# A hybrid sparse-attention encoder in float32: the masks of two tiles built between attention's rows

## What is computed

```python
h = rms_norm(x, gains[0]);  z = h @ w_in        # q k v, indexer q k w, conv B C x, gates A B
score = sum_h wi[h] * relu(qi[h] . ki) ;  score = where(key_chunk <= q_chunk, score, -inf)
_, idx = lax.top_k(score, topk)                 # 256 keys for a prompt row, 40 for a sample row
kg, vg = k[idx], v[idx]
p = softmax(q . kg / 8 over the chosen keys);  o = p @ vg        # 8 query heads, 2 key heads
m = sigmoid(ga) * (o @ w_attn_out) + sigmoid(gb) * ((cb * conv3(cc * cx)) @ w_conv_out)
x = x + rms_norm(m @ w_o, gains[1])
x = x + rms_norm(square(relu(rms_norm(x, gains[2]) @ w_up)) @ w_down, gains[3])
```

## Time and profile before

| | |
|---|---|
| time, median of 3 runs | 3700.87 us (3700.28 to 3704.8) |
| profiled execution: time, span | 3699.1 us, 3697.3 us |
| TensorE matmuls busy | 3375.3 us, 91% |
| VectorE busy | 1903.4 us, 51% |
| ScalarE busy | 721.0 us, 20% |
| GpSimd busy | 1185.1 us, 32% |
| granted TensorE clock, mean | 0.948 of full speed |
| values matmuls (line 623) | 197.0 us in 368 |
| logits matmuls (line 594) | 169.9 us in 704 |

### The profile page before, as it was taken

The page is one execution under the profiler, slowest core; times in us unless marked ns, Lnnn a source line. Parts: engine busy times, 40 slices in busy tenths (PEclk is TensorE's granted clock), DMA queues, the critical chain, the costliest instruction groups (busy, mean ns, idle before and its releaser), DMA issues.

```text
span 3697.3 us, 48934 instructions
## 1 busy us (share of the span) xinstructions
PE 3375.3 (91%) x19604; PEld 3201.4 (87%) x19604; DVE 1903.4 (51%) x3006; ACT 721.0 (20%) x1113; POOL 1185.1 (32%) x497
## 2 busy tenths in 40 slices
PE   3989997999979999999749899979998799999996
PEld 2989996669969999999739899956798799999996
DVE  4249997644174242424372599976442733323244
ACT  2330112541121010101123201125402200101010
POOL 6013331004334443434350133310044344334441
PEclk9989997999979999999869899979999799999998
DMA  4111222012211111112121112220132111111121
GB/s 165 47 57 42 71 91 98 23 42 99 93 65 46 42 44 45 45 45 91 38 90 53 54 44 76 93 87 24 42 105 100 59 43 43 45 45 45 40 93 59
DMA packets 75359, 233.95 MB, mean 63 GB/s; under 512 B 12816, under 2 KB 25456, under 8 KB 73712
## 3 DMA queue, kind: packets, MB, share of 16 engines
q1 hardware_dynamic: 33552, 122.57, 11.0%
q10 hardware_dynamic: 41696, 109.88, 8.0%
HBM read 176.37 MB, written 56.05 MB: 63 GB/s over the span
## 4 chain that ended last, share of the span: by engine, by line
PE 70%; DVE 23%; issue 3%; ACT 2%; ACTq 1%; POOL 1%; DMA 0%; SPq 0%; DVEq 0%; POOLq 0%
PE PS L410 52%; DVE PASS L1268 11%; PE PS L476 5%; PE PS L623 4%; PE PS L594 3%; PE PS L611 2%; PE PS L506 2%; DVE X L1078 1%; DVE TC L1288 1%; DVE HN L1078 1%; PE PS L446 1%; DVE H L1089 1%; DVE TC L1283 1%; PE PS L490 1%; DVE RANK L1322 1%
## 5 line engine op out<-in xcount | busy, mean ns | idle before, releaser
L410 PE MATMUL PS<-H,W 128*128 128x358 f32 x9792 | 1644.9, 330 | 62.9 <-DVE H L1096 53.6
L410 PEld LDWEIGHTS PS<-H,W 128*128 128x128 f32 x9792 | 1635.0, 191 | 69.7 <-ACT H L1011 39.8
L346 POOL TENSOR_TENSOR W<-RAW,ones 128x1024 fp32r<-128x1024 f32 x216 | 419.3, 1941 | 2314.8 <-PE PS L410 1940.6
L410 PE MATMUL PS<-A,W 128*128 128x358 f32 x5760 | 950.0, 327 | 0.0
L410 PEld LDWEIGHTS PS<-A,W 128*128 128x128 f32 x5760 | 948.4, 189 | 1.5 <-issue 1.5
L348 POOL TENSOR_TENSOR W<-RAW,W 128x1024 fp32r<-128x1024 f32 x216 | 613.1, 2838 | 16.9
L1268 DVE TENSOR_SCALAR_CACHE_REDUCE PASS<-SC,TC,CST 48x176 bf16<-48x176 f32 x496 | 408.7, 882 | 2.2
L1457 DVE TENSOR_TENSOR X<-X,PS 128x1074 f32 (+1 forms) x64 | 81.5, 1274 | 593.7 <-PE PS L410 593.7
L476 PE MATMUL PS<-WQ,H 128*128 128x364 f32 (+1 forms) x1296 | 238.4, 340 | 49.0 <-DVE H L1089 19.1
L476 PEld LDWEIGHTS PS<-WQ,H 128*128 128x128 f32 (+1 forms) x1296 | 211.8, 184 | 64.7 <-issue 35.6
L1445 DVE TENSOR_TENSOR SQ<-SQ,RS 128x1074 f32<-128x1074 f32 x64 | 118.1, 1845 | 259.3 <-ACT SQ L1024 258.8
(11 more groups left out here) (133 smaller groups left out, 2274.7 us busy)
## 6 DMA issues: line engine op xcount, KB each, us to landing
RAW<-in_w_slab SPq DMA_DIRECT2D x216, 512.0 KB, 3.6
x_keep<-X ACTq DMA_DIRECT2D x32, 537.0 KB, 2.8
gates<-GS ACTq DMA_DIRECT2D x32, 537.0 KB, 2.9
XT<-x_keep ACTq DMA_DIRECT2D x8, 2148.0 KB, 12.6
RAW<-in_w_qkv SPq DMA_DIRECT2D x16, 546.0 KB, 3.7
GA<-gates ACTq DMA_DIRECT2D x16, 537.0 KB, 3.6
GB<-gates ACTq DMA_DIRECT2D x16, 537.0 KB, 4.5
qs_keep<-QH ACTq DMA_DIRECT2D x16, 512.0 KB, 2.6
```

The source lines that it names most:

```text
L346: g_.tensor_tensor(hi, raw, one, ALU.mult).then_inc(hi_split, 1)
L410: mm = nc.tensor.matmul(PS[:, b0 + c, 0:CW], W[:, s, w, k, :], act[:, a, k, c * CW:(c + 1) * CW], start=(first and w == 0 and a == 0), sto ...
```

## The change

The loop over masks is cut in four functions. The masks of tiles 8 and 1 to 5 are still built before attention, those of tiles 6 and 7 in eight parts within it: one part after `mask_row(i + 2, 1)` and ahead of `normalise(i + 1, 1)` in each of the loop's turns i = 6 to 13. TensorE's waits for `mask0`, `topk_step` and `v_ones` go; VectorE, which alone reads the masks, makes them in its own order. The 1024 keys are loaded in two pieces, 256 and 768, with the q loads between. V loses its columns of ones, and the values matmuls have 64 output rows. `RANK` moves to the memory that V leaves, and `PB` is packed by the group's own row length so that it does not reach the scores of tiles 6 and 7 while these are needed.

```diff
@@ prob, V, RANK @@
-        PB = at("PB", [P, GROUP, LONG], F32, r_x)
+        PB = at("PB", [P, GROUP * LONG], F32, r_x)
...
         def prob(i, g):
 
-            return PA[:, i % 3 * GROUP + g, :] if i % 3 < 2 else PB[:, g, :]
-
-        V = at("V", [P, 10, NKV, P], F32, r_q)
+            e = EXT[ORDER[i // NKV]]
+            return PA[:, i % 3 * GROUP + g, :] if i % 3 < 2 else PB[:, g * e:(g + 1) * e]
+
+        V = at("V", [P, 10, NKV, HD], F32, r_q)
...
-        RANK = at("RANK", [P, EXT[7]], F32, r_q + 10 * 256 * 4)
+        RANK = at("RANK", [P, EXT[7]], F32, r_q + 10 * NKV * HD * 4)
@@ TensorE @@
                 pe.wait_ge(v_put, (l + 1) * 9)
-                pe.wait_ge(v_ones, l + 1)
                 pe.wait_ge(past_in, (l + 1) * 32)
-                pe.wait_ge(mask0, (l + 1) * 2)
-                pe.wait_ge(topk_step, (l + 1) * N_TOPK)
...
-                        if a < 2:
-                            pe.wait_ge(ks_in[a], (l + 1) * 16)
+                        if a in (0, 1, 3):
+                            pe.wait_ge(ks_in[(a + 1) // 2], (l + 1) * 16)
...
-                    nc.tensor.matmul(PS[:, 6 + kv, 0:GROUP * m], V[0:w, vt, kv, :],
+                    nc.tensor.matmul(PS[0:HD, 6 + kv, 0:GROUP * m], V[0:w, vt, kv, :],
@@ ScalarE @@
-                for i, cols in enumerate((slice(META0, NKEY), slice(0, META0))):
+                for i, cols in enumerate((slice(META0, NKEY), slice(0, 2 * P), slice(2 * P, META0))):
                     act.dma_start(KS[:, :, cols].bitcast(F32), d["ks_keep"][:, :, cols]).then_inc(ks_in[i], 16)
                     q_load(i)
-                q_load(2)
@@ VectorE @@
-                V_.memset(V[:, :, :, HD:P], 1.0).then_inc(v_ones, 1)
...
-                for c, t in enumerate(RANKED):
-                    m, e = ROWS[t], EXT[t]
-                    mask, eq, rank = MB[0:m, MB_OFF[t]:MB_OFF[t] + e], SB[0:m, 0:e], RANK[0:m, 0:e]
+                def mask_views(t):
+                    m, e, c = ROWS[t], EXT[t], RANKED.index(t)
+                    return m, e, c, MB[0:m, MB_OFF[t]:MB_OFF[t] + e], SB[0:m, 0:e], RANK[0:m, 0:e]
+
+                def mask_count(t):
+
+                    m, e, c, mask, eq, _ = mask_views(t)
                     kth = TC[0:m, c:c + 1].bitcast(F32)
                     did(V_.tensor_scalar(mask, row(t), kth, cst["negk"][0:m, c:c + 1], ALU.is_gt, ALU.add,
                                          accum_out=CNT[0:m, c:c + 1]))
                     did(V_.tensor_scalar(eq, row(t), kth, None, ALU.is_equal))
                     settled()
+
+                def mask_rank(t):
+
+                    m, e, c, _, eq, rank = mask_views(t)
                     did(V_.tensor_scalar(NEED[0:m, c:c + 1], CNT[0:m, c:c + 1], -1.0, None, ALU.mult))
...
                         did(V_.tensor_tensor_scan(rank, eq, eq, 0.0, ALU.add, ALU.max))
                     settled()
+
+                def mask_keep(t):
+
+                    m, e, c, mask, eq, rank = mask_views(t)
                     did(V_.scalar_tensor_tensor(eq, rank, NEED[0:m, c:c + 1], eq, ALU.is_le, ALU.mult))
                     settled()
                     did(V_.scalar_tensor_tensor(mask, mask, 1.0, eq, ALU.subtract, ALU.add))
                     settled()
+
+                def mask_big(t):
+
+                    mask = mask_views(t)[3]
                     did(V_.tensor_scalar(mask, mask, BIG, None, ALU.mult))
                     settled()
+
+                for t in RANKED[:-2]:
+                    mask_count(t)
+                    mask_rank(t)
+                    mask_keep(t)
+                    mask_big(t)
...
                         if g == 0 and i:
                             outputs(i - 1)
+                        if g == 1 and 6 <= i < 14:
+                            (mask_count, mask_rank, mask_keep, mask_big)[(i - 6) % 4](RANKED[-2 + (i - 6) // 4])
                         if g == 2 and i > 1:
```

More of the change, by code:

```diff
@@ L203, in build @@
         assert SC_COLS * 2 <= 2 * NKEY * 4
-        RANK = at("RANK", [P, EXT[7]], F32, r_q + 10 * 256 * 4)
+        RANK = at("RANK", [P, EXT[7]], F32, r_q + 10 * NKV * HD * 4)
+        assert 10 * NKV * HD + EXT[7] <= 10 * 256
         PT = at("PT", [P, 3, 512], F32, r_q + 10 * 256 * 4)
@@ L270, in build @@
         cache_out = sem("cache_out")
-        v_put, v_ones = sem("v_put"), sem("v_ones")
+        v_put = sem("v_put")
         turned, turned_out = sem("turned"), sem("turned_out")
@@ L279, in build @@
         conv_tap = sem("conv_tap")
-        qs_in, ks_in = [sem("qs_in0"), sem("qs_in1"), sem("qs_in2")], [sem("ks_in0"), sem("ks_in1")]
+        qs_in, ks_in = [sem("qs_in0"), sem("qs_in1"), sem("qs_in2")], [sem("ks_in0"), sem("ks_in1"), sem("ks_in2")]
         logit_done, masked, tail_masked = sem("logit_done"), sem("masked"), sem("tail_masked")
@@ L792, in _ @@
                 act.wait_ge(rs_bcast, l * 4 + 1)
-                act.dma_start(V[:, 9, :, 0:HD], d["past_v"][bass.ds(l, 1)].rearrange("a p x n -> p (a x) n"))\
+                act.dma_start(V[:, 9, :, :], d["past_v"][bass.ds(l, 1)].rearrange("a p x n -> p (a x) n"))\
                    .then_inc(past_in, 16)
@@ L834, in put_v @@
                     act.wait_ge(sb_copied, nn + 1)
-                    copy(V[0:m, t, :, 0:HD], SB[0:m, C_V:C_IW].rearrange("p (v c) -> p v c", v=NKV))\
+                    copy(V[0:m, t, :, :], SB[0:m, C_V:C_IW].rearrange("p (v c) -> p v c", v=NKV))\
                         .then_inc(v_put, 1)
@@ L1327, in _ @@
                     settled()
+                def mask_big(t):
+                    mask = mask_views(t)[3]
                     did(V_.tensor_scalar(mask, mask, BIG, None, ALU.mult))
                     settled()
-                assert k_[0] == N_TOPK, (k_[0], N_TOPK)
+                for t in RANKED[:-2]:
[3 more added lines that the diff above has]
+                    mask_big(t)
                 dve.wait_ge(gates_stored[0], (l + 1) * 8 * 16 + 16)
@@ L1404, in _ @@
                 o_lo_part(9 * NKV - 1)
+                assert k_[0] == N_TOPK, (k_[0], N_TOPK)
                 with dve.Fori(0, NMERGE // 2) as g:
```

## The result

| | before | changed |
|---|---|---|
| time, median of 4 runs | 3702.73 us (3700.28 to 3704.8) | 3746.02 us (3740.26 to 3747.87) |
| profiled execution: time, span | 3699.1, 3697.3 us | 3740.26, 3738.5 us |
| attention, layer 0: begins, takes | 608.68, 201.3 us | 597.34, 238.3 us |
| attention, layer 1: begins, takes | 2447.50, 205.1 us | 2457.89, 235.2 us |
| values matmuls, busy | 197.0 us in 368 | 213.7 us in 368 |

The ratio is 1.0115, with a 95% interval of 1.0097 to 1.0132. The prediction, 3691 us with a range of 3681 to 3701, was wrong, and with the chance of 0.03 for slower it was sure of itself as well.

A forecast was written before the change was run, and what follows sets the result against it. TensorE, busy 91% of the span, bounds the kernel, so only its idle stretches can yield gain. Per layer 12.3 - 4.6 - 2.8 = 4.9 us, 9.8 in all: 3699.1 to 3689.3, plus 1.8 for the median: 3691 us, range 3681 to 3701.

The forecast's parts named there:

- V without ones: Values matmuls in attention: still 512 columns each, shorter weight loads have nothing to shorten; 0, up to 1 us a layer gain.
- The wait that goes: Ahead of attention's first logits: TensorE's 20 us mask wait ends, logits begin at 596.4; gain 12.3 us a layer.
- Keys in pieces: Key loads at attention's start: no wait for group 2's logits; cost 0, bounds -1 to +1 us a layer.
- The mask parts: VectorE in attention, turns 6 to 13: parts delay normalised rows beyond idle time; cost 4.6 us a layer, bounds 2.5 to 14.3.
- The clock: TensorE in attention: longer waits ahead of groups 7 to 9 bring 1.8 new falls; cost 2.8 us a layer.
- Covered parts: Rival in attention: VectorE's gaps take the masks, no new falls; 8.8 us a layer gained, 3683 us; chance 0.20.
- the low stretch of over 25 us at the start: Sign of being wrong: TensorE's low-clock stretch as attention starts exceeds 25 us; it was 21.5 and 22.4.
- More falls, slower: Rival in attention: waits starting groups 7 to 14 each bring a clock fall; 3710 to 3716 us; chance 0.03.
- Shorter weight loads: Rival at the values matmuls: half of V's columns shorten each step some 0.1 us; 3673 us; chance 0.04.
- The start is held: Rival at attention's start: clock rises by time, not place of work; 0.8 us a layer lost, 3702 us; chance 0.13.

The follow-up runs named there:

- full-width twin of the change: The changed kernel with both key heads' V side by side as one 128-column weight, no ones, each head's own 64 output rows read: 3699.86 us, ratio 0.9985.
- late-parts version: The full-width twin of the change with each mask part moved from ahead of the second normalise to behind the third of its turn: 3692.2 us, ratio 0.9964.

## Why the prediction was wrong

**The step that failed is "V without ones", costed at 0 with up to 1 us a layer to gain.** It argued that a values matmul takes the time of its 512 columns whatever the weights, and that the weight loads lie under other work, so that shorter ones have nothing to shorten. The first holds for a narrow matmul behind a narrow one (0.43 us each with narrow and with full weights). The second held before and not after: at each border between 128 and 64 columns the load begins only with its own matmul. Left out was thus what stands beside the narrow matmul. At a step's two borders 0.29 us is lost: 1.59 for 1.30. In 72 of a layer's 92 steps that is new, 21 us a layer and 42 in both; sixteen paid it before, and the special tile's four hardly show it. The rest came by the clock: 43.3 and 24.2 us more at the low level, which at the 0.46 us of the earlier trace rows are 31 us. Together that is 73 us where attention took 67 longer; the terms overlap somewhat, and 0.46 is a price from another mix of steps. Undone alone, the step is worth 46 us in the changed kernel (3699.9) and 73 in the kernel before (3777.1 less 3704.3); of the 27 us between the two, 21 are the clock's (39 us of low time against 84, at 0.46).

The sign was in the trace, and I passed it over: the steps of the 16-key tile take 1.58 us beside 1.30, though they do the same columns with fewer rows. I read the form that occurs 122 times in the earlier trace rows and bounded the narrower one from it, below at nothing.

The Trainium skill bears on it where I cited only its page on the clock: "TensorEngine Tiling (Array Packing)", section "Tiling Modes", gives 128x64 as a division of its own and says that changing the mode, as opposed to the tile, drains TensorE. If a plain matmul with narrow weights is such a mode, which that section does not say, weights of up to 64 columns between full ones pay twice a step. The runs agree at three points: 64 columns pay and 96 don't, a repeat of the same form pays nothing, and 16 rows pay until they are filled to 128. They give 0.29 us for both borders. Its section "Restrictions" adds that column tiling excludes the transposes of float32; the trace agrees, as the transposes with 16 columns are followed by values after 0.43 us, like the wide ones. That the load at a border waits for the matmul ahead of it fits a drain, but no run here shows the drain itself, so that it is one is the page's word; that it is the border and not the width is shown.

**The wait that goes: right, but for layer 1.** Start forecast 596.4, measured 597.34; a wait of 7.1 us for q stands there. That is 11.3 us in layer 0, not 12.3. In layer 1 the wait is 12.9 us shorter, but 1.26 come back right behind the start as a wait for VectorE: the remaining masks are not ready first there, as the prediction took them to be.

**Keys in pieces: right,** at 0, for the change. Without the piece there is a wait of 2.7 and 1.1 us, not 0.3, though the time does not show it.

**The mask parts: right in sum, wrong in how.** Forecast 4.6 us a layer; at quick steps the edit costs 8.5 us in both. But the waits grew by only 2.5 us in layer 0, where turn 6 cost nothing (0.83 for the 1.4 that I gave group 7), turn 7 made 1.45 for 1.9 and turn 8 1.04 for 1.4. VectorE's idle time moves along when it is late and covers more than gap by gap. By all waits inside attention it is 2.4 and 2.9 us, 5.3 in both. The rest is the clock's: low time is 13.4 us more in layer 0 and 7.9 less in layer 1, net 5.5, or 2.5 us at 0.46. In the changed kernel's layer 0 the parts cost nothing: its slow steps hide them (waits of 0.94 and 1.01, as before).

**The clock: wrong in size, and not by the rule I used.** I expected 1.8 new falls a layer, 5.9 us at the low level, behind the parts' waits. In the full-width twin of the change the windows where groups 7 and 8 begin, layer 0, show two of them, 3.4 and 3.5 us:

```profile
661.00:675.00 14.00, 13.05 (x63) 9.06 (x60) 9.54 (x26) 6.75 (x16) 0.00 (x0) 0.88 0.03 5
674.00:690.00 16.00, 13.76 (x64) 9.18 (x62) 11.82 (x31) 6.78 (x16) 0.00 (x0) 0.89 0.11 34
```

The version with the 16-key tile filled too has the same parts at the same places, and the waits above; its clock is full from ahead of group 7 to attention's end:

```profile
660.00:799.53 139.53, 134.35 (x661) 88.84 (x661) 90.95 (x218) 84.45 (x166) 0.00 (x0) 1.00 0.04 12
```

So these waits of about 1 us did not bring a fall by themselves. Each group begins, right behind that wait, with the 16-key step; that its borders decide is what the pair suggests, but one profile of each does not show it. In the twin low rose by 18.7 and 10.1 us over before, at 0.46 us each 13 us in both for my 5.6. That and the parts' waits (5 us) make 18 of the 20.5 us by which its attention takes longer, and these leave 4 of the 24 to 25 us that the starts bring. The late-parts version has the waits of before and is 27 us more at the low level all the same: what an earlier start changes there is not explained.

**The rivals.** "Covered parts", whose 3.5 us a layer the prediction does not derive, fits the changed kernel's layer 0 and is refuted where the steps are quick. Of the prediction's own signs of being wrong one came, the low stretch of over 25 us at the start. "More falls, slower" had the sign by another cause: even the twin with its falls behind the waits was not slower than before. The section that it leans on, "HAM oscillation — how this bites in real kernels" of the Trainium skill's "TensorE: Matmul & The Clock Gate", tells of waits for transfers that are longer than any inside attention of the two kernels, so it did not speak for this rival. "Shorter weight loads" had the right edit and the wrong sign; by the rule that it cites from the same page, section "Step-by-step: what each phase is for", that the time of a load scales with the columns, the loads would have halved, and they went from 200 to 145 ns. "The start is held" is refuted by the full-width kernels, whose first low stretch stays at 21 to 25 us with 12 us less waiting ahead of it. Where the masks stay ahead of attention and TensorE waits 12.3 and 15.3 us behind its first logits, the stretch is 36 and 38 us, longer by about that wait: it ends at the same place of the work.

## What to carry to other kernels

Before narrowing a matmul's weights because half of the output is unused, look at what stands beside it on TensorE, and compare the starts of successive groups where the trace already has a narrow or a short form; a full-width weight with useless columns or zero rows can be the faster one. Where two edits share a step, price the one that "does less work" as carefully as the one that adds some, and read "issue" before the weight loads. A wait is worth removing only if what it waits for leaves the path of the next engine too.

## What the runs showed of the hardware that I had not expected

- Transposes (128 columns) and values matmuls in turn: 1.30 us with 128 and 96 columns, 1.59 with 64; 16 rows of 128 pay 0.28 too, and 0.38 with logits in the step. At such a border the weight load begins with its own matmul, elsewhere 0.1 to 0.4 us ahead of it. Filling the unused part with zeros is worth 20 to 26 us in this kernel.
- The granted clock stayed at the low level for 48 us of attention with TensorE busy 94% of them by the profile, and for 21 us when the same work stood in full-width weights; with each values matmul issued twice, still narrow, it was 27 us. The profile's busy share did not tell when it would rise. Whether the borders or the narrow content held it is open.
- With weights full in columns and rows, no kernel had a low stretch later than some 60 us into attention, with the parts' waits or without; nor had the kernel before, with its 16-row steps. With 64 columns they came up to 97 us in the changed kernel and 100 in the kernel before with narrow weights. With 128 or 96 columns, 16-row steps and an early start they came up to 103 us, and at 124 to 134 in two kernels. Why so late is open.
